# Roots by token, a 256-key window and a reordered start, in a two-block model kernel on one core

## What is computed

```python
def rms_norm(x, g): return x * rsqrt(mean(x * x, -1) + 1e-6) * g

# first block, both layers: heads of 64 features are normed one by one
q = apply_rope(rms_norm(q, q_norm_g), cos, sin) * 64 ** -0.5     # 8 heads
k = apply_rope(rms_norm(k, k_norm_g), cos, sin)                  # 2 heads

# RWKV branch, end: each head of 64 features is centred and scaled by its own root
y = (y - mean) * rsqrt(var + 64e-5) * ln_w + ln_b
y = (y + bonus) * g                                              # g = sigmoid(gd) @ g_up

# neighbourhood attention: 512 tokens are a grid of 8 rows by 64 columns, 16 heads of 64
z = rmsnorm(h, na_norm) @ na_w_qkv
q = rmsnorm(heads(z[:, :D]), q_g) * 64 ** -0.5;  k = rmsnorm(heads(z[:, D:2*D]), k_g)
# a query at grid column c sees all 8 rows and the 16 columns from clip(c - 8, 0, 48)
p = softmax(q @ k_window + rpb[h, row distance, column distance])
h = h + (p @ v_window) @ na_w_out

# per-layer embedding, both layers
h = h + sigmoid(rmsnorm(h, ple_norm) @ w_gate) * (p_i @ w_proj)  # p_i has 256 features
```

## Time and profile before

| | us |
|---|---|
| median of 3 runs | 3958.33 |
| lowest and highest | 3956.54 and 3960.83 |
| the profiled execution's own time | 3957.86 |
| its span, first to last instruction | 3956.5 |

### The profile page before, as it was taken

The page is one execution under the profiler, slowest core; times in us unless marked ns, Lnnn a source line. Parts: engine busy times, 40 slices in busy tenths (PEclk is TensorE's granted clock), DMA queues, the critical chain, the costliest instruction groups (busy, mean ns, idle before and its releaser), DMA issues. The chain is left out here.

```text
span 3956.5 us, 54401 instructions
## 1 busy us (share of the span) xinstructions
PE 3471.2 (88%) x23106; PEld 2353.7 (59%) x23106; DVE 1902.5 (48%) x2854; ACT 1119.3 (28%) x1869; POOL 285.1 (7%) x223
## 2 busy tenths in 40 slices
PE   7689889998878979999796777779999897899998
PEld 6367533332727644333285766647888684478887
DVE  3564433222365442322346545556663532966645
ACT  3353300000344320000133222114333421743333
POOL 1010000000101000000011222100000100200000
PEclk9899989999989989999898888979999997999999
DMA  5022179999202128999721000012222222322222
GB/s 201 11 86 86 68 297 428 427 428 424 94 6 107 64 88 362 427 427 428 318 96 44 3 3 2 3 40 91 107 85 80 91 107 43 57 80 97 107 75 75
DMA packets 78841, 599.31 MB, mean 151 GB/s; under 512 B 35124, under 2 KB 37428, under 8 KB 43336
## 3 DMA queue, kind: packets, MB, share of 16 engines
q1 hardware_dynamic: 78600, 595.84, 38.0%
HBM read 593.72 MB, written 2.10 MB: 151 GB/s over the span
## 5 line engine op out<-in xcount | busy, mean ns | idle before, releaser
L577 PE MATMUL psum<-source_hi,weights_hi 128*128 128x512 f32 (+1 forms) x2352 | 923.0, 392 | 99.8 <-DVE weights_lo L487 75.7
L577 PE MATMUL psum<-source_lo,weights_hi 128*128 128x512 f32 (+1 forms) x2352 | 912.9, 388 | 0.0
L577 PE MATMUL psum<-source_hi,weights_lo 128*128 128x512 f32 (+1 forms) x2352 | 911.8, 388 | 0.0
L577 PEld LDWEIGHTS psum<-source_hi,weights_hi 128*128 128x128 f32 x2352 | 449.6, 191 | 201.3 <-DVE weights_lo L487 90.1
L577 PEld LDWEIGHTS psum<-source_lo,weights_hi 128*128 128x128 f32 x2352 | 449.9, 191 | 90.5 <-issue 2.9
L577 PEld LDWEIGHTS psum<-source_hi,weights_lo 128*128 128x128 f32 x2352 | 449.4, 191 | 89.9
L1398 PE MATMUL psum<-weight_ring_first,branches 128*64 128x512 f32 x2048 | 467.2, 599 | 14.4 <-DMA weight_ring_first<-in_w_up 7.6
L487 DVE TENSOR_TENSOR weights_lo<-weight_ring_second,weights_hi 128x1024 fp32r<-128x1024 f32 (+3 forms) x230 | 286.1, 1248 | 288.1 <-ACT weights_hi L442 288.0
L1398 PEld LDWEIGHTS psum<-weight_ring_first,branches 128*64 128x64 f32 x2048 | 138.4, 137 | 303.8 <-issue 274.3
L442 ACT CAST weights_hi<-weight_ring_second 128x1024 fp32r<-128x1024 f32 (+3 forms) x230 | 228.1, 997 | 262.0 <-PE psum L577 235.6
L1551 DVE TENSOR_TENSOR x<-psum,x 128x512 f32<-128x512 f32 x256 | 164.1, 685 | 204.9 <-PE psum L1431 204.9
(11 more groups left out here) (353 smaller groups left out, 4447.5 us busy)
## 6 DMA issues: line engine op xcount, KB each, us to landing
weight_ring_first<-in_w_gate SPq DMA_DIRECT2D x64, 2048.0 KB, 16.1
weight_ring_first<-in_w_up SPq DMA_DIRECT2D x64, 2048.0 KB, 17.9
lent_weights<-in_w_down SPq DMA_DIRECT2D x64, 2048.0 KB, 17.0
weight_ring_second<-in_ffn_w_up SPq DMA_DIRECT2D x22, 2048.0 KB, 7.9
weight_ring_first<-in_xattn_w_kv SPq DMA_DIRECT2D x8, 2048.0 KB, 7.7
weight_ring_second<-in_ffn_w_down SPq DMA_DIRECT2D x8, 2048.0 KB, 7.9
weight_ring_first<-in_w_in SPq DMA_DIRECT2D x6, 2048.0 KB, 23.4
weight_ring_second<-in_mix_w_in SPq DMA_DIRECT2D x6, 2048.0 KB, 8.6
```

What stands on the lines that cost most here:

```text
L577: ins = pe.matmul(ps, a, b, start=k == 0 and q == 0, stop=k == job.rows // P - 1 and q == 2)
```

## The change

- **`head_norms`** takes its sums by token: `sum_heads` issues four matmuls a tile, each with 128 tokens of squares as weights and two columns of ones; the root and the reciprocal are on 128 partitions by eight columns a tile, one pair of instructions for q and one for k; `spread_heads` issues eight matmuls a tile, each 64 by 128. The three table loads and the wait for them are gone. `rwkv_finish` does likewise, and its fourth gate product moves behind the spreads.
- **`near_attention`** takes the place of `paired_attention(window=True)`. Tokens are stored by grid column, so that the 128 queries of a tile need 256 keys. Bias and mask come as one host-made table, one DMA of 512 KB a pair. Each step has two score matrices of 128 by 256, four transposes, one copy; the output takes 16 matmuls of 64 by 128 a pair. There are four probability buffers instead of three, and DVE's and ACT's look-ahead is two steps.
- **`qkv`** of that layer reads its source and writes q and k in the new token order (`view`, `keep_qkv`).
- **Staggered start** of `ask` (the cross attention's query job, both layers) and of `qkv`: the first two units run over source tiles 0 to 6, then each takes tile 7, and what follows a unit (the spread) comes behind both.
- **`proj`**'s weight is one piece of 1 MB.

```diff
+def sum_heads(pe, K, to, src):
+
+    for t in range(TT):
+        ins = pe.matmul(to[:, 2 * t:2 * t + 2], src[:, t * P:(t + 1) * P], K.ones_head[:, 0:P:HALF], start=True, stop=True)
+    return ins
...
+            for i, (_, _, m) in enumerate(items):
                 pe.wait_ge(sq_act if i % 2 else sq_ready, i // 2 + 1)
-                pe.matmul(K.psum[0:rows, 0, :], ones_at[:, rows - 2 * i:2 * rows - 2 * i], sq[:, i % 4, :],
-                          start=i == 0, stop=i == n - 1).then_inc(summed, 1)
-            pe.wait_ge(inverse, 1)
-            for i in range(n):
-                if i >= 7:
-                    pe.wait_ge(scaled, i - 6)
-                pe.matmul(K.psum[:, 1 + i % 7, :], back[:, i * P:(i + 1) * P], root[:, :], start=True, stop=True)\
-                    .then_inc(spread, 1)
+                at = (i - first[m]) * TT * 2
+                sum_heads(pe, K, K.psum[:, m, at:at + 2 * TT], sq[:, i % 4, :]).then_inc(summed, 1)
+            for i, (_, _, m) in enumerate(items):
+                pe.wait_ge(inverse, m + 1)
+                if i >= 6:
+                    pe.wait_ge(scaled, i - 5)
+                spread_heads(pe, K, K.psum[:, 2 + i % 6, :], root[:, i]).then_inc(spread, 1)
...
-            dve.wait_ge(root_ready, 1)
-            dve.reciprocal(root[:, :], root[:, :]).then_inc(inverse, 1)
-            for i, (src, gain) in enumerate(items):
+            for m in range(len(parts)):
+                dve.wait_ge(root_ready, m + 1)
+                dve.reciprocal(root[:, of_part(m)], root[:, of_part(m)]).then_inc(inverse, 1)
+            for i, (src, gain, _) in enumerate(items):
                 dve.wait_ge(spread, i + 1)
-                dve.scalar_tensor_tensor(out=src, in0=src, scalar=gain, in1=K.psum[:, 1 + i % 7, :],
+                dve.scalar_tensor_tensor(out=src, in0=src, scalar=gain, in1=K.psum[:, 2 + i % 6, :],
...
+        u = 0
+        while u < len(self.units):
+            unit = self.units[u]
+            n = len(unit.ks)
+            if unit.job.staggered and u == unit.job.begins:
+                other = self.units[u + 1]
+                product(unit, range(n - 1), False)
+                product(other, range(n - 1), False)
+                product(unit, range(n - 1, n), True)
+                product(other, range(n - 1, n), True)
+                after(unit)
+                after(other)
+                u += 2
+            else:
+                product(unit, range(n), True)
+                after(unit)
+                u += 1
...
-            for t in range(4):
+            for t in range(3):
                 pe.matmul(K.psum[:, 4 + t, :], g_up[:, t * P:(t + 1) * P], sg[:, :], start=True, stop=True).then_inc(gates, 1)
             for t in range(4):
                 pe.wait_ge(squared, t + 1)
-                pe.matmul(K.psum[:, t, :], K.ones_head, tmp[:, t, :], start=True, stop=True).then_inc(var, 1)
+                sum_heads(pe, K, K.psum[:, 7, 2 * TT * t:2 * TT * (t + 1)], tmp[:, t, :]).then_inc(var, 1)
+            pe.wait_ge(inverse, 1)
+            for t in range(4):
+                spread_heads(pe, K, K.psum[:, t, :], scale[:, t]).then_inc(spread, 1)
+            pe.matmul(K.psum[:, 7, :], g_up[:, 3 * P:4 * P], sg[:, :], start=True, stop=True).then_inc(gates, 1)
...
-    proj = Job(lambda k: p[:, k, :], 256, [feature(), feature()], lambda i, act, ps, link, r: act.copy(pp[:, i, :], ps),
+    proj = Job(lambda k: p[:, k, :], 256, [columns_of(D)], lambda i, act, ps, link, r: act.copy(pp[:, i, :], ps),
...
+            def score(j):
+                p, qt = divmod(j, TT)
+                if j >= 2:
+                    pe.wait_ge(biased, 2 * (j - 1))
+                for a in range(2):
+                    tiles = k[rows(a), p, :].rearrange("p (s t) -> p s t", t=P)
+                    keys = tiles[:, qt:qt + 2, :] if qt < TT - 1 else tiles[:, 0:TT:TT - 1, :]
+                    ins = pe.matmul(K.psum[:, 2 * (j % 2) + a, 0:W], q[rows(a), p, qt * P:(qt + 1) * P], keys,
+                                    start=True, stop=True)
+                ins.then_inc(scores, 1)
+
+            def turn(j):
+                if j >= 2:
+                    pe.wait_ge(turned_kept, j - 1)
+                for a in range(2):
+                    pe.wait_ge(prob_ready, 2 * j + a + 1)
+                    for s in range(2):
+                        at = (2 * a + s) * P
+                        ins = pe.transpose(K.psum[:, 4 + j % 2, at:at + P], prob[:, j % 4, a, s * P:(s + 1) * P], K.ident)
+                ins.then_inc(turned, 1)
+
+            def out(p):
+                pe.wait_ge(turned_kept, TT * (p + 1))
+                if p >= 2:
+                    pe.wait_ge(out_kept, p - 1)
+                for qt in range(TT):
+                    for s, tile in enumerate(key_tiles(qt)):
+                        for a in range(2):
+                            ins = pe.matmul(K.psum[rows(a), 6 + p % 2, qt * P:(qt + 1) * P],
+                                            v[:, tile, (2 * p + a) * HEAD:(2 * p + a + 1) * HEAD],
+                                            probT[:, p % 2, qt, a, s, :], start=s == 0, stop=s == 1)
+                ins.then_inc(out_ready, 1)
+
+            score(0)
+            score(1)
+            for j in range(n):
+                if j + 2 < n:
+                    score(j + 2)
+                turn(j)
+                if j % TT == 0 and j:
+                    out(j // TT - 1)
+            out(pairs - 1)
...
+            def row_max(j):
+                b = j % 4
+                p, qt = divmod(j, TT)
+                dve.wait_ge(scores, j + 1)
+                dve.wait_ge((landed0, landed1)[p % 2], 16 * (p // 2 + 1))
+                if j >= 4:
+                    dve.wait_ge(turned, j - 3)
+                for a in range(2):
+                    dve.tensor_tensor_reduce(out=prob[:, b, a, :], in0=K.psum[:, 2 * (j % 2) + a, 0:W],
+                                             in1=table[:, p % 2, qt // (TT - 1), a, :], scale=1.0, scalar=-3.0e38,
+                                             op0=ALU.add, op1=ALU.max, accum_out=st[:, b, a:a + 1]).then_inc(biased, 1)
+                dve.wait_ge(biased, 2 * (j + 1))
+                dve.tensor_scalar(st[:, b, NMAX], st[:, b, MAX], -1.0, None, ALU.mult).then_inc(nmax_ready, 1)
...
+            row_max(0)
+            row_max(1)
+            for j in range(n):
+                if j + 2 < n:
+                    row_max(j + 2)
+                b = j % 4
+                dve.wait_ge(exp_done, 2 * (j + 1))
+                link(dve.reciprocal(st[:, b, INV], st[:, b, SUM]))
+                for a in range(2):
+                    dve.tensor_scalar(prob[:, b, a, :], prob[:, b, a, :], st[:, b, 6 + a:7 + a], None, ALU.mult)\
+                        .then_inc(prob_ready, 1)
...
-                grid = lambda a: a.rearrange("p (r c) -> p r c", c=GRID_W)
-                if i < KT:
-                    return eng.tensor_tensor(grid(q[:, i, :])[:, :, ::-1], grid(ps), grid(r[0]), ALU.mult)
+                cut = lambda a: a.rearrange("p (c r) -> p c r", c=GRID_W)
                 if i < 2 * KT:
-                    return eng.tensor_tensor(k[:, i - KT, :], ps, r[0], ALU.mult)
+                    root = by_rows(r[0])
+                    if i >= KT:
+                        return eng.tensor_tensor(cut(k[:, i - KT, :]), cut(ps), root, ALU.mult)
+                    to = cut(q[:, i, :])
+                    eng.tensor_tensor(to[:, GRID_W - 8:, :], cut(ps)[:, 0:8, :], root[:, 0:8, :], ALU.mult)
+                    return eng.tensor_tensor(to[:, 0:GRID_W - 8, :], cut(ps)[:, 8:, :], root[:, 8:, :], ALU.mult)
...
-        out += col_pieces(dram["ple_w_proj_2"][l], 256, D)
+        out += col_pieces(dram["ple_w_proj_2"][l], 256, D, wide=D)
```

More of the change, by code:

```diff
@@ L448, in source @@
             self.slot_free(act, t)
-            to, src = self.xhi[:, t % self.slots, 0:job.n_tok], job.src(k)[:, 0:job.n_tok]
+            there, here = job.view
+            to, src = there(self.xhi[:, t % self.slots, 0:job.n_tok]), here(job.src(k)[:, 0:job.n_tok])
             if job.gain is None:
@@ L495, in source @@
             job, k = self.tiles[t]
-            hi, lo = (a[:, t % self.slots, 0:job.n_tok] for a in (self.xhi, self.xlo))
-            src = job.src(k)[:, 0:job.n_tok]
+            there, here = job.view
+            hi, lo = (there(a[:, t % self.slots, 0:job.n_tok]) for a in (self.xhi, self.xlo))
+            src = here(job.src(k)[:, 0:job.n_tok])
             dve.wait_ge(self.src_hi, t + 1)
@@ L554, in bank_free, with product @@
                 self.kept(pe, job, i)
-        for unit in self.units:
+        def product(unit, ks, finish):
             job = unit.job
-            if unit.ends_piece:
-                pe.wait_ge(self.ring.used, unit.piece + 1)
-            else:
-                pe.wait_ge(self.w_lo, unit.lo)
+            if ks[0] == 0:
+                if unit.ends_piece:
+                    pe.wait_ge(self.ring.used, unit.piece + 1)
```

(20 more changed lines are left out.)

241 lines of the change are left out of this document (135 added, 106 removed).

## The result

| | before | after |
|---|---|---|
| median | 3959.58 (3956.54 to 3964.86, 4 runs) | 3932.07 (3928.78 to 3934.72, 4 runs) |
| span of the profiled execution | 3956.5 | 3929.6 |
| mean granted clock | 0.939 | 0.930 |

The ratio is 0.9929, with a 95% interval of 0.9912 to 0.9946: 0.5 to 0.9% faster. The forecast was 3928.3, range 3897 to 3948. To see where the 26.9 us of span come from I set the same instructions of the two traces against each other and read how much earlier each stretch runs, at points between the stages. The table gives, for each place, by how much that lead changes there; minus is time won.

The account below looks back on a forecast made before the run. PE, busy for 88% of the span, was taken to bound the kernel nearly everywhere. Terms of -9.5, -8.0, -11.8, -3.6, -6.4 and +9.3 sum to -30.0 us, giving 3928.3 us, range 3897 to 3948.

Parts of the forecast that it names:

- the first block: Head norms in both layers: no wait for tables, sums by token, root and reciprocal of q hidden; -9.5 us together.
- qkv: Start of qkv: the stagger removes PE's 1.87 us wait for source tile 7; -3.6 us (0 to -5).
- the loop: Neighbourhood attention: DVE and PE form one chain per step, mostly at the low clock; stage 141.1 us, +9.3.
- rwkv_finish: Four reciprocals of 3.35 us go, sums by token, spreads hidden under DVE's work; -8.0 us.
- gate: Start of gate, two layers: its first piece is issued 16 us earlier, so PE runs on from proj; -11.8 us.
- the neighbourhood layer's head norms: Head norms before the attention loop: more instructions traded for no gap and a higher clock; -6.4 us.
- signs of being wrong: Missing DVE wait before the row maximum, a loop clock of 1.00, or a gap moving to an unnamed place.
- P: Attention loop, time of one step's chain of DVE and PE work: 2.94 us at 2.4 GHz, 3.69 at 1.2 GHz.
- O: Attention loop, output in the chain once a pair: about 1.95 us at 2.4 GHz, 3.68 at 1.2 GHz.
- The quarter: Attention loop: a quarter of the time at the higher clock, giving P = 3.50, O = 3.45, stage 141.1 us.
- keeps 2.4 GHz: Rival: the attention loop stays at 2.4 GHz, -18.6 us in place of +9.3, kernel 3900.4; chance 0.2.
- slower than before: Rival: attention loop's products no longer overlap, a step costs 0.43 to 0.85 us more, kernel 3953 to 3980; chance 0.04.

Follow-up runs that it names:

- e2_busy: The changed kernel with four extra identity matmuls ahead of each attention step's transposes, in PE's waits: 3907.13, ratio 0.9871 to the kernel before.
- e1_look1: The changed kernel with DVE's row maximum and ACT's exponential one step ahead instead of two: 3873.3, ratio 0.9785 to the kernel before.
- e8_ple_rwkv: The kernel before with only proj's weight as one piece and the new rwkv_finish: 3938.93, one run.
- e3_head: The kernel before with the new head_norms alone, in all three uses: 3938.03, ratio 0.9952.
- e5_read: The changed kernel with one-step look-ahead, qkv's source reordered by strided read and contiguous write instead of strided write: 3873.87.
- e4_stagger: The kernel before with the staggered start of ask and qkv alone, source read as before: 3954.25, one run.
- e10_nostagger: The changed kernel with one-step look-ahead and output a step at a time, qkv's stagger taken out, strided reorder kept: 3870.64.
- e9_plain: The changed kernel with one-step look-ahead and output a step at a time, without the reorder of qkv's source tiles: 3855.47, ratio 0.9735.

## Why the prediction was right, point by point

**The sum is closer than its terms.** Forecast and median are 3.8 us apart. Against the table, the first block, `qkv` and the loop came out 2.5, 4.9 and 2.3 us worse than put, `rwkv_finish`, `gate` and the neighbourhood layer's head norms 2.1, 1.0 and 3.1 better. The mechanisms of most places were right; that errors of 9.7 and 6.2 us nearly cancel is luck. One of the prediction's own signs of being wrong also came up: idle time of PE grew at places that it hadn't named, ahead of the first block's scores and ahead of `qkv`.

**Attention loop: right, with the mechanism.** P was put at 3.69 and O at 3.68 for 1.2 GHz; they were 3.87 and 3.68. At 2.4 GHz P was put at 2.94 and O at 1.95; e2_busy shows 3.00 and e1_look1's outputs 1.97. The stage was put at 141.1 and took 142.2. The mix of clocks came out as put: a granted 0.62 is a quarter of the way from 0.50 to 1.00, and behind the outputs the trace has steps of 2.9 to 3.3 us between those of 3.87. The quarter was an estimate between two rows, so that it came out this closely is in part luck. One slip is in the sum: a quarter of the time at the higher clock gives O = 3.25, not 3.45, and a stage of 139.5; the eight outputs took 3.46 on average. The rival "keeps 2.4 GHz" was excluded by the trace, and e1_look1 and e2_busy show both ways to get a higher clock. The rival "slower than before" wanted at least 0.43 us more a step; the step was 0.18 over P.

**`gate`: right** (-12.8 for -11.8), and e8_ple_rwkv gives it alone.

**`rwkv_finish`: right in its mechanism, 1.4 us low.** DVE's last instruction ends 15.9 us behind the start of the sums, where the working had 16.5; the sums took 3.89 and not 4.5, and the spreads stayed hidden. The term left out is the fourth gate product: moved behind the spreads, it no longer stands ahead of the sums, which start 0.9 us earlier for it (2.74 us of gate products instead of 3.60). Together that is the 9.4 us by which DVE's work in this stage got shorter. The table's 10.1 is read at PE's products on either side and holds 0.3 us ahead of the stage and 0.3 behind it.

**Head norms of the neighbourhood attention: the term of the sums was 3.3 us too long.** The working gave all 128 records 0.22. The first ones still ran fast; PE comes to them after 1.6 us of idle time now, not 5.8:

```profile
3271.00:3274.70 3.70, 3.10 (x28) 3.10 (x28) 2.06 (x4) 1.61 (x3) 0.00 (x0) 0.99 0.00 0
...
3281.00:3296.00 15.00, 15.00 (x71) 15.00 (x72) 2.63 (x4) 2.09 (x4) 0.00 (x0) 0.50 0.01 1
```

28 records in 3.10 us are 0.11 each at 0.99, 71 in 15 are 0.21 at 0.50. How many run fast is not fixed by that idle time alone: with the same 1.6 us it was 27 here, 31 in e3_head and 13 in e5_read, and the sums took 24.8, 24.3 and 26.1 us. This also settles the weighed rule of the Trainium skill ("TensorE: Matmul & The Clock Gate", "LDWEIGHTS (loading the stationary operand)"). For 128 columns it gives 0.107 us a load. The trace agrees at the full clock (0.11 a record) and not at 0.50 (0.21): with the same 128 columns the pitch follows the clock, which the rule leaves out. The spreads were 16.92, put at 16.8. The bound of -15 for fast sums was put too close: by the working's own numbers it is -6.4 less 128 times 0.08, which is -16.6.

**First block's head norms: the gain at the stage's end was as put (-5.1 and -5.3, for -4.6 and -4.9), but 1 to 2 us were given back behind it.** The step that failed is that the working stopped at the stage. Five swap matmuls follow, then rotary work on DVE with PE idle. The swaps now run at the full clock (4.53, before 7.42), and PE stands idle for longer ahead of the scores. The first eight records of scores are slow in both kernels; the next four and their transposes run at 1.2 GHz now, where before they ran at 2.4. Before, then after:

```profile
161.88 3.78 PE L906 MATMUL psum<-qk 64*128 64x512 f32 x8 [7.92 <-PEq L124]
166.96 1.13 PE L906 MATMUL psum<-qk 64*128 64x512 f32 x4 [1.29 <-ACT probs L992]
...
156.02 3.78 PE L924 MATMUL psum<-qk 64*128 64x512 f32 x8 [10.86 <-PEq L124]
161.09 2.08 PE L924 MATMUL psum<-qk 64*128 64x512 f32 x4 [1.29 <-ACT probs L994]
```

That the longer idle time keeps the clock down is my reading; layer 2 shows the same (10.79 us idle for 8.55, 2.08 for 1.13), but no run isolates it.

**`qkv`: wrong, -3.6 against +1.3.** The stagger is worth what was put (e4_stagger -4.1, e10_nostagger 5.0). The step that failed is the parenthesis on strided source reads, "may take back 2": it was sized too small, and it is missing from the -3.6. The casts on ACT and DVE, each 0.4 to 0.6 us longer, decide when PE can start, and they also delay the weights of `gate`'s last units: 5.3 us in all (e9_plain). -4.1 and 5.3 make the +1.3 of the table to 0.1 us. The longer stores of the new order (1.07 to 1.10 instead of 0.69 us for a tile of k) cost nothing: e9_plain has them and e4_stagger doesn't, and both take 140.3 us from `gate`'s last product to the last of `qkv`.

**What went unnoticed:** the first products behind the loop start in a slow stretch now (a granted 0.50 in their first 3.2 us, before 0.72), which costs 1.2 us and is in the row of the loop in the table.

## What to carry to other kernels

Halving the work of the bounding engine pays only if its overlap with the others stays: write down for one step which instruction waits for which, in each engine's order, before and after. A look-ahead is right when what it asks for stands in the other engine's queue *ahead* of the instruction that waits for this engine's previous result; one step more, with the other queue left as it was, made a pipeline into a chain (142 us), one step less made it 82. Split a block of matmuls that serves a whole group into steps, when another engine waits for what is queued behind it. And cost a reorder by what waits for it: strided casts of 1.2 us instead of 0.7 cost 5.3 us here, since they stood ahead of a product's start and between the casts of the weights that PE needed next.

## What the runs showed of the hardware that I had not expected

- Added matmuls can shorten a kernel: with 128 useless ones in PE's waits its granted clock in the loop rose from 0.62 to 0.97, and the time fell by 25 us (e2_busy).
- A strided access costs nearly the same on the read and on the write side: a cast of 128 by 512 took 1.18 to 1.28 (ACT) and 1.13 to 1.34 us (DVE) with strided writes, 1.16 to 1.22 and 1.08 to 1.18 with strided reads, 0.72 and 0.75 with none.
- A faster stage can be followed by a slower one: 3 us won in five swap matmuls became idle time of PE, and four records of scores behind it took 2.08 instead of 1.13 us.
- A weight load of 128 columns with a matmul of two columns behind it had a pitch of 0.11 us at a granted 0.99 and of 0.21 at 0.50.
